# Expert weights loaded in quarters, released pair by pair three ahead, with semaphores by buffer

## What is computed

```
for l in range(2):
    h = rms_norm(x);  proj = h @ w_in[l]
    x = x + w_out( sigmoid(gA) * P_A(windowed attention, 8 heads, 2 kv) + sigmoid(gB) * P_B(dilated mixture, 3 x 4 heads) )
    t = rms_norm(x)
    group  = argmax(t @ w_rg + b_rg)                   # 4 groups, top 1
    top 2 experts of that group's 8, softmax weights   # 32 experts
    a, u = t @ w_g[e], t @ w_u[e]                      # 1024 x 256 each
    x = x + sum_e combine[e] * ((silu(a) * u) @ w_d[e])   # 256 x 1024
return rms_norm(x)
```

## Time and profile before

| | us |
|---|---|
| median of 3 runs | 1300.89 |
| lowest and highest | 1299.39, 1300.89 |
| the profiled execution | 1300.83 |
| its span, first to last instruction | 1298.9 |
| TensorE busy | 1195.1 (92%) |
| VectorE busy | 589.1 (45%) |
| ScalarE busy | 409.3 (32%) |
| GpSimd busy | 241.5 (19%) |
| mean DMA rate over the span | 236 GB/s |

### The profile page before, as it was taken

The page is one execution under the profiler, slowest core; times in us unless marked ns, Lnnn a source line. Parts: engine busy times, 40 slices in busy tenths (PEclk is TensorE's granted clock), DMA queues, the critical chain, the costliest instruction groups (busy, mean ns, idle before and its releaser), DMA issues.

```text
span 1298.9 us, 17626 instructions
## 1 busy us (share of the span) xinstructions
PE 1195.1 (92%) x6456; PEld 797.3 (61%) x6456; DVE 589.1 (45%) x1420; ACT 409.3 (32%) x818; POOL 241.5 (19%) x179
## 2 busy tenths in 40 slices
PE   7999999999999999889599999989999999978971
PEld 6777787888886333323287777778888853433320
DVE  5667765444345232112456687553344442322115
ACT  5444456333342011001244444563333411100002
POOL 1315420222200111111022244102221001111100
PEclk9999999999999999889899999999999999999996
DMA  5323321653676999999833333026537769999995
GB/s 207 113 82 98 99 82 36 210 208 97 242 233 249 395 423 425 426 420 411 320 106 94 94 102 101 34 91 222 174 100 292 260 240 423 423 423 425 418 411 217
DMA packets 68960, 306.03 MB, mean 236 GB/s; under 512 B 11862, under 2 KB 12246, under 8 KB 58128
## 3 DMA queue, kind: packets, MB, share of 16 engines
q1 hardware_dynamic: 58288, 282.97, 57.7%
q0 software_dynamic: 10304, 21.23, 4.5%
q10 hardware_dynamic: 288, 0.77, 0.2%
HBM read 289.16 MB, written 23.07 MB: 240 GB/s over the span
## 4 chain that ended last, share of the span: by engine, by line
PE 68%; DMA 14%; SPq 7%; DVE 4%; ACT 3%; issue 2%; DVEq 1%; POOLq 0%; ACTq 0%
PE bank L566 14%; PE bank L568 14%; PE bank L567 14%; DMA gu<-in_gu_w 12%; PE bank L897 10%; SPq L407 5%; PE bank L914 4%; PE bank L696 2%; SPq L412 2%; PE bank L725 2%; PE bank L660 1%; DMA raw<-in_stream 1%; PE bank L829 1%; PE bank L892 1%; DMA yld<-y_rows 1%
## 5 line engine op out<-in xcount | busy, mean ns | idle before, releaser
L897 PE MATMUL bank<-gu,xgt 128*64 128x512 f32 x976 | 227.9, 616 | 39.5 <-DMA gu<-in_gu_w 38.3
L566 PE MATMUL bank<-h_hi,w_hi 128*128 128x512 f32 x640 | 254.4, 398 | 3.4 <-DVE h_lo L1340 1.9
L568 PE MATMUL bank<-h_hi,w_lo 128*128 128x512 f32 x640 | 249.7, 390 | 0.0
L567 PE MATMUL bank<-h_lo,w_hi 128*128 128x512 f32 x640 | 249.4, 390 | 0.0
L897 PEld LDWEIGHTS bank<-gu,xgt 128*64 128x64 f32 x976 | 70.5, 141 | 191.1 <-issue 142.3
L1305 DVE TENSOR_TENSOR w_lo<-raw,w_hi 128x1024 fp32r<-128x1024 f32 x100 | 131.6, 1317 | 120.6 <-ACT w_hi L1028 120.4
L566 PEld LDWEIGHTS bank<-h_hi,w_hi 128*128 128x128 f32 x640 | 120.5, 188 | 29.8 <-issue 3.3
L568 PEld LDWEIGHTS bank<-h_hi,w_lo 128*128 128x128 f32 x640 | 120.3, 188 | 25.7
L567 PEld LDWEIGHTS bank<-h_lo,w_hi 128*128 128x128 f32 x640 | 120.6, 188 | 23.6
L914 PE MATMUL bank<-dn,zt 128*64 128x512 f32 x512 | 116.9, 598 | 6.0 <-ACT zt L1262 2.8
L1028 ACT ACTIVATE w_hi<-raw 128x1024 fp32r<-128x1024 f32 x100 | 105.2, 1052 | 46.3 <-PE bank L568 42.9
(11 more groups left out here) (210 smaller groups left out, 1661.5 us busy)
## 6 DMA issues: line engine op xcount, KB each, us to landing
gu<-in_gu_w SPq DMA_DIRECT2D x18, 4096.0 KB, 31.2
raw<-in_stream SPq DMA_DIRECT2D x112, 512.0 KB, 3.7
dn<-in_dn_w SPq DMA_DIRECT2D x18, 2048.0 KB, 34.8
gu<-in_gu_w SPq DMA_DIRECT2D x26, 1024.0 KB, 19.2
dn<-in_dn_w SPq DMA_DIRECT2D x20, 1024.0 KB, 19.3
gu<-in_gu_w SPq DMA_DIRECT2D x32, 512.0 KB, 5.3
swp<-pj SPq DMA_DIRECT2D x136, 64.0 KB, 2.6
dn<-in_dn_w SPq DMA_DIRECT2D x16, 512.0 KB, 5.3
```

The costliest lines, as they stand in the source:

```text
L566: mm(dst, ah, bh, start=start, stop=False)
L567: mm(dst, ah, bl, start=False, stop=False)
L568: return mm(dst, al, bh, start=False, stop=stop)
L897: last = mm(bank[b][e * CAP:(e + 1) * CAP, :], xgt[:, x_s, k, e * CAP:(e + 1) * CAP], gu[w_s][:, e, k, :] if not early or k < 2 else gu_up ...
```

## The change

Every pair from 2 on is now in `PARTS` with quarters. TensorE increments one semaphore, `w_free`, after k = 1, 3 and 5 of the up stage of each pair from 1 to 12, after k = 1 and 3 of pair 0, and after the first half of pair 0's down stage; SP waits for these counts (`FREED`) before each quarter, and for `gu_ok` before the last one. The first half of pair 3's `dn` is released by pair 0's first half. The second quarter of pair 4 for expert 1 goes to `gu_mid[1]` once pair 0's k = 3 is done, and the matmuls read it there (`gate_up`). Parts share semaphores by buffer (`slot_gu`, `slot_dn`), with running counts from `landings` and `dn_landings`. Pair 0's down stage, and those of pairs 4 to 12, run with f in the outer loop. The first pair's rows: a new semaphore `xgh_ok` is released after k = 3 of the last tile of tokens, DVE scales the first half then, the second half after `xgt_ok`, and only then the slots of pair 1.

```diff
-PARTS = {2: 4, 3: 4, PAIRS - 3: 2, PAIRS - 2: 4, PAIRS - 1: 4}
+PARTS = {n: 4 for n in range(2, PAIRS)}
+FREED = {(0, 1): 1, (0, 3): 2, **{(n, k): 3 * n + 1 + k // 2 for n in range(1, PAIRS - RING) for k in (1, 3, 5)}}
+FREED_DN, FREES = 3, 3 * (PAIRS - RING)
+def pieces(p, q):
+    return 2 if (p == 3 and q) or (p, q) == (4, 1) else 1
+def landings(l, p, q):
+    same = [n for n in range(2, PAIRS) if n % RING == p % RING]
+    return l * sum(pieces(n, q) for n in same) + sum(pieces(n, q) for n in same if n <= p)
+def dn_landings(l, p):
+    same = [n for n in range(2, PAIRS) if n % RING == p % RING]
+    return l * len(same) + same.index(p) + 1
...
+        slot_gu = [sems(*(f"slot_gu{s}_{q}" for q in range(4))) for s in range(RING)]
+        slot_dn = [sems(*(f"slot_dn{s}_{f}" for f in range(2))) for s in range(RING)]
...
-                sp.wait_ge(gu_free, l + 1)
+                sp.wait_ge(w_free, l * FREES + FREED[0, 1])
                 load_gu_part(l, 3, 0)
+                sp.wait_ge(w_free, l * FREES + FREED[0, 3])
+                sp.dma_start(gu_mid[1].rearrange("p k n -> p (k n)"),
+                             gu_w[bass.ds(l * PAIRS + 4, 1), 1, :, 2 * 2 * FE:4 * 2 * FE].rearrange("o p n -> p (o n)")).then_inc(gu_part[4][1], 16)
+                sp.wait_ge(w_free, l * FREES + FREED_DN)
+                load_dn_part(l, 3, 0)
                 sp.wait_ge(dn_ok, l * PAIRS + 1)
-                load_dn_part(l, 3, 0)
                 load_dn_part(l, 3, 1)
                 for p in range(4, PAIRS):
-                    sp.wait_ge(gu_ok, l * PAIRS + p - RING + 1)
...
                         for q in range(PARTS[p]):
-                            load_gu_part(l, p, q)
+                            if p >= 4:
+                                end = (q + 1) * (KD // PARTS[p]) - 1
+                                if end < KD - 1:
+                                    sp.wait_ge(w_free, l * FREES + FREED[p - RING, end])
+                                else:
+                                    sp.wait_ge(gu_ok, l * PAIRS + p - RING + 1)
+                            if (p, q) == (4, 1):
+                                sp.dma_start(gu[1][:, 0, 2:4, :].rearrange("p k n -> p (k n)"),
+                                             gu_w[bass.ds(l * PAIRS + 4, 1), 0, :, 2 * 2 * FE:4 * 2 * FE].rearrange("o p n -> p (o n)")).then_inc(gu_part[4][1], 16)
+                            else:
+                                load_gu_part(l, p, q)
...
+                        if (t, k) == (TT - 1, 3):
+                            last.then_inc(xgh_ok, 1)
...
+                def gate_up(n, w_s, e, k):
+                    if n == 0 and k >= 4:
+                        return gu_up[:, e, k - 4, :]
+                    if k in (2, 3) and (n == 0 or (n, e) == (4, 1)):
+                        return gu_mid[e][:, k - 2, :]
+                    return gu[w_s][:, e, k, :]
...
-                            pe.wait_ge(gu_part[n][k // w], (l + 1) * (32 if n == 3 and k >= 2 else 16))
+                            pe.wait_ge(gu_part[n][k // w], landings(l, n, k // w) * 16)
...
-                        if n == 0 and k == 1:
-                            last.then_inc(gu_free, 1)
+                        if (n, k) in FREED:
+                            last.then_inc(w_free, 1)
...
+                    elif n == 0:
+                        landed(first_dn, dn_ld, n)
+                        for f in range(2):
+                            for half in range(2):
+                                last = down_step(0, half, f)
+                            last.then_inc(w_free if f == 0 else dn_ok, 1)
...
+                dve.wait_ge(xgh_ok, l + 1)
+                turned(0, xtd_ok, (0,))
                 dve.wait_ge(xgt_ok, n0 + 1)
-                turned(0, xtd_ok, (0,))
+                turned(0, xtd_ok, (1,))
                 dve.wait_ge(inf_ok, n0 + 1)
                 slots(1, ix_ok)
-                turned(0, xtd_ok, (1,))
```

More of the change, by code:

```diff
@@ L316, in hybrid_encoder @@
         gu_ld, dn_ld = sems(*(f"gu_ld{i}" for i in range(RING))), sems(*(f"dn_ld{i}" for i in range(RING)))
-        gu_part = {p: sems(*(f"gu_part{p}_{q}" for q in range(n))) for p, n in PARTS.items()}
-        dn_part = {p: sems(*(f"dn_part{p}_{f}" for f in range(2))) for p in PARTS}
-        gu_free, up_ld = sems("gu_free", "up_ld")
+        slot_gu = [sems(*(f"slot_gu{s}_{q}" for q in range(4))) for s in range(RING)]
+        slot_dn = [sems(*(f"slot_dn{s}_{f}" for f in range(2))) for s in range(RING)]
+        gu_part = {p: slot_gu[p % RING] for p in PARTS}
+        dn_part = {p: slot_dn[p % RING] for p in PARTS}
+        w_free, up_ld = sems("w_free", "up_ld")
         sel_ok, inf_ok, ix_ok, xgt_ok, xtd_ok = sems("sel_ok", "inf_ok", "ix_ok", "xgt_ok", "xtd_ok")
+        xgh_ok = sem("xgh_ok")
         xg_ld, ysc = sems("xg_ld0", "xg_ld1"), sems("ysc0", "ysc1")
@@ L491, in _ @@
                 load_mid(l, 0, up_ld)
-                sp.wait_ge(gu_free, l + 1)
+                sp.wait_ge(w_free, l * FREES + FREED[0, 1])
                 load_gu_part(l, 3, 0)
+                sp.wait_ge(w_free, l * FREES + FREED[0, 3])
[3 more added lines that the diff above has]
+                load_dn_part(l, 3, 0)
                 sp.wait_ge(dn_ok, l * PAIRS + 1)
-                load_dn_part(l, 3, 0)
                 load_dn_part(l, 3, 1)
                 for p in range(4, PAIRS):
-                    sp.wait_ge(gu_ok, l * PAIRS + p - RING + 1)
+                    if p < 4:
+                        sp.wait_ge(gu_ok, l * PAIRS + p - RING + 1)
                     if p in PARTS:
                         for q in range(PARTS[p]):
-                            load_gu_part(l, p, q)
+                            if p >= 4:
[3 more added lines that the diff above has]
+                                else:
+                                    sp.wait_ge(gu_ok, l * PAIRS + p - RING + 1)
+                            if (p, q) == (4, 1):
[3 more added lines that the diff above has]
+                                load_gu_part(l, p, q)
                     else:
@@ L893, in turn, with up_step @@
                     last.then_inc(done, 1)
-                def up_step(b, x_s, w_s, k, early=False):
+                def gate_up(n, w_s, e, k):
[4 more added lines that the diff above has]
+                    return gu[w_s][:, e, k, :]
+                def up_step(b, x_s, w_s, k, n=None):
                     for e in range(2):
-                        last = mm(bank[b][e * CAP:(e + 1) * CAP, :], xgt[:, x_s, k, e * CAP:(e + 1) * CAP],
-                                  gu[w_s][:, e, k, :] if not early or k < 2 else gu_up[:, e, k - 4, :] if k >= 4 else gu_mid[e][:, k - 2, :],
+                        last = mm(bank[b][e * CAP:(e + 1) * CAP, :], xgt[:, x_s, k, e * CAP:(e + 1) * CAP], gate_up(n, w_s, e, k),
                                   start=k == 0, stop=k == KD - 1)
@@ L953, in up_pair @@
                         if n in PARTS and k % w == 0:
-                            pe.wait_ge(gu_part[n][k // w], (l + 1) * (32 if n == 3 and k >= 2 else 16))
+                            pe.wait_ge(gu_part[n][k // w], landings(l, n, k // w) * 16)
                         if n == 0 and k == 2:
                             pe.wait_ge(up_ld, (l + 1) * 48)
-                        last = up_step(n % 2, n % 2, n % RING, k, n == 0)
-                        if n == 0 and k == 1:
-                            last.then_inc(gu_free, 1)
+                        last = up_step(n % 2, n % 2, n % RING, k, n)
+                        if (n, k) in FREED:
+                            last.then_inc(w_free, 1)
                     last.then_inc(gu_ok, 1)
@@ L969, in down_pair @@
                         for f in range(2):
-                            pe.wait_ge(dn_part[n][f], (l + 1) * 16)
+                            pe.wait_ge(dn_part[n][f], dn_landings(l, n) * 16)
                             for half in range(2):
```

## The result

The changed kernel took 1304.57 us (median of 20 runs, 1301.12 to 1308.35) where the kernel before took 1301.48 (20 runs). The ratio is 1.0019 with a 95% interval of 1.0011 to 1.0027: by it the change is slower by 2.5 us, 1.4 to 3.5. The forecast was 1299.2, a gain of 1.6. The profiled execution took 1304.30, its span is 1302.4 us, 3.5 over before.

The account below looks back on a forecast made before the run. The prediction took the landing of expert weights over full DMA engines as the bound; per layer, lead 4.9 + 0.5 less 4.3 gave 1.1, taken as 0.8, so 1300.83 - 1.6 = 1299.2 us, range 1292.5 to 1304.5.

Parts of the forecast that it names:

- What bounds the kernel: Expert stages: each ends when its weights have arrived; only release before about 436 us can gain.
- One sign named beforehand: End of the first layer's expert stage: the last quarter's matmuls would start at 624 to 626 us.
- Part 1: Start of each expert stage: earlier release of pairs 3 and 4 gives a lead of 4.9 us a layer.
- Part 2: First pair's rows: scaling by halves starts pair 0 earlier, 0.5 us a layer; the later first gather stays hidden.
- Part 3: Weight loads of pairs 4 to 13: 4 KB runs at 411 GB/s cost 4.3 us a layer.
- The sum: Per layer: lead 4.9 + 0.5, less 4.3, is 1.1; 0.8 taken, 1.6 in two layers.
- The cross-check by all bytes: First layer's expert stage: all weight bytes at 411 GB/s end at 621.9 us, not 622, a gain of 0.1.
- B: Full stretch: gathers and scatters sharing engines with 4 KB runs push the rate under 409 GB/s; 1304.0 to 1305.8 us; chance 0.2.
- my forecast's own band: Full stretch: 409 to 414 GB/s with a lead of about 5, by itself 1296 to 1301 us; chance 0.57.
- C: Start of expert stages: release misses the DMA or first gather is late, lead 4 or less; 1301.4 us; chance 0.08.
- A: Weight loads: quarters as fast as whole copies, only the lead is left; 1290.0 us, or 1294.3; chance 0.15.
- What costs nothing: SP's extra issues (6 a pair, not 2) and PE's added waits in the expert stages cost no time.

Follow-up runs that it names:

- e1: The changed kernel with early release kept for pairs 3 and 4, but pairs 5 to 12 as single copies and pair 13 in halves; 1294.77 us.
- e12: e1 with the first pair's rows scaled as in the kernel before, without halves; 1295.49 us.
- e2: The changed kernel with quarters everywhere, but weights released late as in the kernel before and no piece fetched ahead; 1311.34 us.
- e6: The changed kernel with gu weights and buffers laid out so gu quarters have 8 KB runs, dn still 4 KB; 1297.85 us.
- e5: The kernel before with each single copy of pairs 4 to 12 split in two by expert, runs unchanged; 1302.28 us.
- e10: The changed kernel with both gu and dn laid out so that every run is 8 KB; 1295.88 us.
- e11: e8 with pairs 5 to 12 in halves instead of single copies, 16 KB runs for gu and 8 KB for dn; 1293.02 us.
- e8: e1 with weights and buffers laid out so all runs double, whole gu 32 KB and whole dn 16 KB; 1301.94 us.

## Why the prediction was wrong, step by step

**What bounds the kernel: right.** Both stretches end with the landing of the last quarter, before and after, and e1 shows that what is sent before 436 us comes back at the end nearly whole. One sign named beforehand came late: the last quarter's matmuls of the first layer start at 626.10, in a profile in which everything from the row matmuls on starts 1.56 us earlier than in before, so they are outside 624 to 626.

**Part 1, a lead of 4.9 us: this is where the prediction failed.** With the 0.5 of part 2 it was 5.4; e1 and e12 have 3.4 to 3.8 by the stretches, 3.2 to 3.4 by the times, from which the dearer runs of pair 4 are already taken, as they were in my sum. Two terms were too kind. The first half of dn went out at 418.22, and I had the engines full 1.4 us later; the windows show 115 GB/s in 418 to 421 and 395 after it, so 0.35 MB by 421 instead of 0.6, which is 0.6 us. And I charged 0.7 us to the kernel before for "the second gather's rest". In its trace that gather is issued at 423.26 and lands 7.4 us later, at 430.7, when gu of pair 4 had by my own sum only just begun, at 430.5: 0.2 us are left of the 0.7. These two and the 0.5 of part 2 are 1.6 us, and 5.4 less 1.6 is 3.8.

**Part 2, 0.5 us from the halves: failed.** The wait for xgt did go, as predicted. But "pair 0 starts 0.5 us earlier" was the whole step, and what is late next was not asked of pair 0's own weights: steps 2 and 3 come from gu_mid. In both kernels SP issues that copy 2.8 us after the row matmuls begin (404.42 here, 405.97 before), since it waits for the stores of h_rows to land (10.3 us here), and in the changed kernel PE stands until 3.8 us after the issue. DVE's earlier scaling moves none of this. The price that I feared, the later gather, did not show: PE waits for no gather in either profile.

**Part 3, a price of 4.3 us: right in kind, and in size as far as the runs tell.** They give 4.3 to 5.4. The rate was 410 where I took 411, and the windows of single copies alone give 422 to 423. Pair 13, whose halves of 8 KB runs became quarters of 4 KB, I named and charged nothing; at 410 against 417 GB/s its 6.3 MB are 0.3 us, an estimate. "2.8% less than the mixture" was a slip: 411 is 2.8% under the large copies alone (422.7) and 2.4% under the mixture (421).

**The sum.** 5.4 - 4.3 = 1.1, of which I took 0.8, was a difference of two terms of the same size. By the times it is 3.4 - 4.6 = -1.2 a layer, 2.5 slower in two; by the stretches 3.6 - 5.2 = -1.6, 3.2 slower. (Lead is e1 against before and price the change against e1, so these sums come out by construction. The independent price, e2's 4.7, would give about -1.1, with pair 4 in both terms.) The lead was 1.8 us too large, the price at most 1 too small, and the sign turned. The cross-check by all bytes was the better sum: it gave 0.1. With 410 for 411 (0.5 us), without the 0.5 of the halves and with the engines full 0.6 us later it gives -1.5. The two sums differed by 1.0 a layer from the start, more than the forecast gain of 0.8, and I took a number near the kinder one. The measured median lies 0.07 us above the end of the range.

**The rivals.** B said that the rate would fall under break-even, as gathers and scatters share the engines with 4 KB runs. That extra fall didn't come: 410 in the stretch with gathers, 411 in the last quarters. The break-even rose instead. It was put at 409 GB/s with a lead of 5.4; with 3.6 it is 73.7/(175 + 3.6) = 413, and 410 falls under it. So the change is slower in most of what I had called my forecast's own band, 409 to 414. C had the right number, a lead of 4 or less, by a mechanism that the trace does not show: the releases reach the DMA, from 418 on, and PE waits for no gather. A (quarters as fast as single copies) fails in e2 and e6: the quarters of e6 are as many, and faster with longer runs. By the rule of the Trainium skill that A stood beside (DMA: Bandwidth & Descriptors, Specifications, full line rate from 512 B on) 4 KB runs would have cost nothing; here they cost 2.8% against the large copies (410 GB/s in e2 beside 422 before, over the same 150 us), and the measurement decides.

**What costs nothing: right.** SP stood in the issues of four copies for 13.34 us with no loss at the end; in e5 twice the copies changed nothing. PE's waits for gu in 400 to 635 went from 17.1 us in 12 waits to 20.5 in 22; in layer 2 (1040 to 1285) they stayed at 21, in 20 waits instead of 14. More and shorter waits, as said, and the landing decides.

## What to carry to other kernels

Where the DMA engines are full for a long stretch, a transfer's run length is a price on every byte, and an early release is a gain once: multiply the first by the length of the stretch before cutting copies into pieces. When two ways of adding up differ by as much as the forecast gain, find the term on which they differ before choosing. Cut only the pieces whose early start fills an idle engine (here pairs 3 and 4), or lay the data out so that a piece is still one long run. When a forecast is the difference of two near equal terms, give it the width of both. After taking away a wait, look at every other operand of the same instruction.

## What the runs showed of the hardware

The price is per run and small. The change adds 19456 packets of weights, so 608 for each of 16 engines and layer; 4.3 to 5.4 us over these are 7 to 9 ns for each. The rates give the same by another way. At 410 GB/s an engine takes 160 ns for a 4 KB run, at 420 (all runs 8 KB, e10) 312 ns for an 8 KB run: 152 ns for each 4 KB and 7.6 ns for each run. From these two numbers the other layouts come out as estimates, and they fit:

| runs, gu and dn | estimated GB/s | measured |
|---|---|---|
| 8 and 4 KB (e6) | 417 | 417 |
| 16 and 8 KB (before, e5, e11) | 423 | 422 to 423 |
| 32 and 16 KB (e8) | 427 | 426 to 427 |

Runs can also be too long. With 32 KB runs beside them, gathers went from 8.9 to 15.1 us from issue to landing (the median), and the kernel lost all that it had won; with 16 KB they took 9.4, with 8 KB 8.2 and with 4 KB 7.1. They move rows of 4 KB each, on another queue than the weights. The Trainium skill (DMA: Bandwidth & Descriptors, Queues, rings and completion order) says that each engine goes round its queues and changes over only at the end of a packet. These landing times, growing with the runs of the other queue, fit that; no run here shows the turns themselves.
